# An expert stage written out over 16 pairs, with eight weight slots and gathers in the middle of the pairs

## The reference

```
def hier_moe(xn, w_rg, b_rg, w_re, b_re, w_gate, w_up, w_down):
    ...                       # top-1 of 4 groups, top-2 of 8 experts in it
    def expert_block(args):
        xb, e = args
        hdn = jax.nn.silu(xb @ w_gate[e]) * (xb @ w_up[e])
        return hdn @ w_down[e]
    ...
    y_sorted = y_pad[dest] * gate_flat[order][:, None].astype(y_pad.dtype)
    out = jax.ops.segment_sum(y_sorted, tok_sorted, num_segments=t)
```

## Time and profile before

| | us |
|---|---|
| median of three runs | 1980.41 |
| the profiled execution, its own time | 1979.28 |
| its span | 1977.5 |
| TensorE busy | 1767.3 (89%) |
| VectorE, ScalarE, GpSimd busy | 707.9, 669.3, 666.8 |
| DMA read | 524.25 MB, mean 266 GB/s over the span |

### The profile page before, as it was taken

How to read it: one execution, slowest core, us unless ns; L and a number is a source line. 1 busy time by engine, 2 the same in 40 slices (tenths; PEclk the granted TensorE clock), 3 DMA queues, 4 the chain that set the end, 5 groups by cost and what they waited for, 6 DMA issues and landing times.

```text
span 1977.5 us, 27621 instructions
## 1 busy us (share of the span) xinstructions
PE 1767.3 (89%) x8814; PEld 1074.9 (54%) x8814; DVE 707.9 (36%) x1299; ACT 669.3 (34%) x1300; POOL 666.8 (34%) x537
## 2 busy tenths in 40 slices
PE   6999999996988989889779999999969889898897
PEld 5789666785333333333267896667853333333432
DVE  5538667323112121121255385773241121211211
ACT  4565555653111111111145555566421011110200
POOL 6688565893000000000066885558920000000000
PEclk9999999997999999999989999999979999999999
DMA  7344221463799998989553541215538989989895
GB/s 282 128 171 171 86 69 60 154 272 143 310 427 382 429 430 363 428 373 430 252 214 134 193 172 58 86 43 205 222 128 359 427 366 430 429 374 428 358 429 243
DMA packets 38022, 526.77 MB, mean 266 GB/s; under 512 B 4232, under 2 KB 5016, under 8 KB 6160
## 3 DMA queue, kind: packets, MB, share of 16 engines
q1 hardware_dynamic: 37504, 523.74, 64.9%
q0 software_dynamic: 400, 1.59, 0.2%
HBM read 524.25 MB, written 1.06 MB: 266 GB/s over the span
## 4 chain that ended last, share of the span: by engine, by line
PE 37%; issue 35%; POOL 13%; DMA 8%; DVE 4%; ACT 1%; POOLq 0%; DVEq 0%; SPq 0%; ACTq 0%
POOL view L1738 12%; PE PS L968 9%; DMA view<-in_w_exp_up_dram 8%; PE PS L995 3%; PE PS L651 3%; PE PS L653 3%; PE PS L652 3%; PE PS L785 2%; PE PS L943 2%; PE PS L745 2%; PE PS L746 2%; PE PS L747 2%; DVE view L1430 2%; PE PS L820 1%; PE PS L794 1%
## 5 line engine op out<-in xcount | busy, mean ns | idle before, releaser
L1738 POOL TENSOR_TENSOR view<-view,view 128x512 fp32r<-128x512 f32 x448 | 578.1, 1311 | 667.3 <-ACT view L1028 662.3
L968 PE MATMUL PS<-view,view 128*64 128x512 f32 x2048 | 466.1, 612 | 62.7 <-DMA view<-in_w_exp_up_dram 41.5
L968 PEld LDWEIGHTS PS<-view,view 128*64 128x64 f32 x2048 | 151.5, 141 | 371.8 <-issue 371.8
L1028 ACT ACTIVATE view<-view 128x512 fp32r<-128x512 f32 x448 | 273.7, 628 | 206.4 <-PE PS L653 189.6
L651 PE MATMUL PS<-view,view 128*128 128x512 f32 x704 | 295.5, 420 | 8.9 <-POOL view L1738 8.6
L653 PE MATMUL PS<-view,view 128*128 128x512 f32 x704 | 275.4, 391 | 0.0
L652 PE MATMUL PS<-view,view 128*128 128x512 f32 x704 | 275.1, 391 | 0.0
L995 PE MATMUL PS<-view,view 128*64 128x512 f32 x1024 | 234.6, 612 | 6.3 <-ACT view L1257 6.3
L1670 DVE TENSOR_TENSOR view<-PS,view 128x512 f32<-128x512 f32 x32 | 22.1, 692 | 498.5 <-PE PS L968 498.5
L651 PEld LDWEIGHTS PS<-view,view 128*128 128x128 f32 x704 | 133.2, 189 | 46.9 <-POOL view L1738 13.2
L652 PEld LDWEIGHTS PS<-view,view 128*128 128x128 f32 x704 | 133.3, 189 | 32.8 <-issue 8.2
(11 more groups left out here) (242 smaller groups left out, 1988.1 us busy)
## 6 DMA issues: line engine op xcount, KB each, us to landing
view<-in_w_exp_gate_dram SPq DMA_DIRECT2D x64, 2048.0 KB, 16.6
view<-in_w_exp_up_dram SPq DMA_DIRECT2D x64, 2048.0 KB, 15.9
view<-in_w_exp_down_dram SPq DMA_DIRECT2D x64, 2048.0 KB, 14.8
view<-in_w_mix_dram SPq DMA_DIRECT2D x56, 2048.0 KB, 7.8
view<-bias_table POOLq DMA_DIRECT2D x1, 1536.0 KB, 15.1
view<-in_x_dram SPq DMA_DIRECT2D x1, 1024.0 KB, 4.9
out_dram<-view SPq DMA_DIRECT2D x1, 1024.0 KB, 4.7
dtw<-in_w_dt_dram SPq DMA_DIRECT2D x2, 256.0 KB, 5.1
```

The costliest lines, as they stand in the source:

```text
L968: ins = pe.matmul(bank(ph, name, j)[s * CAP:(s + 1) * CAP, :], xgT[:, k, (2 * j + s) * CAP:(2 * j + s + 1) * CAP], slot8[first + s][:, k, ...
L1028: nc.scalar.activation(highs(chunk), weights(slot8, chunk), ACT.Copy).then_inc(*high_ready.up(ph))
L1738: g_.tensor_tensor(weights(low8, chunk), weights(slot8, chunk), highs(chunk), ALU.subtract).then_inc(*low_ready.up(ph))
```

## The change

1. The expert part is no longer a loop over four units. Each engine has the 16 pairs of a layer written out, in the same layer program as the mixer (`first_pass` on TensorE); all their fills stand in `MIX_PLAN`. The units remain for the extra passes only, with semaphores of their own (`over_...`).
2. Eight weight slots that rotate: load n goes to slot `ORDER[n % 8]` and is issued once the product that used load n - 8 is complete. The two new slots lie in the memory of hT and the sigmoids (`r_h`, `r_g`) and in that of the bias table and M (`r_bt`, `r_m`). Hence the bias table is loaded anew in each layer, by the sync engine, within the mixer.
3. Gathers are for four experts (256 columns, `HALF`). Those of the next four stand in the middle of a pair, 16 matmuls in each of two pairs, between the first scatter and the transposes of hh. A fill holds two of the eight k blocks; the banks are 7 and 2, and ScalarE copies out the even fills and VectorE the odd ones. VectorE makes the selection ahead, at the start of each even pair.
4. `vectors` for the next layer moves behind load 16; the mixer's first blocks wait for the last g and u instead of u and y2.
5. In the branch not taken VectorE alone raises the semaphores, 27 of them.

```diff
+def gathered(j):
+    return (2 * (j % 2), 2 * (j % 2) + 1) if j // 2 + 1 < HALVES else ()
...
+ORDER = (4, 5, 1, 2, 0, 3, 6, 7)
...
+        slot_at = [region(SLOT) for _ in range(6)]
+        r_h, r_g, r_bt, r_m = region(2 * D), region(2 * D), region(HEADS * 384), region(1024)
+        slot_at += [r_h, r_bt]
...
                 for i, src in enumerate(blocks):
                     if i < RING:
-                        sp.wait_ge(*filled[1 if i < 2 else 4].at(ph, 0))
+                        sp.wait_ge(*filled[0 if i else 1].at(ph, 0))
...
+                    if i == RING + 1:
+                        sp.wait_ge(*filled[4].at(ph, 0))
+                        sp.wait_ge(s_skew, 16)
+                        sp.dma_start(BT, bass.AP(table_dram.tensor, 0, [[1, P], [WIN, HEADS], [1, 384]])
+                                     ).then_inc(*bt_in.up(ph))
...
+                sp.wait_ge(*full(ph, "lg"))
+                load(1, 0, 0)
+                load(1, 0, 1)
+                for n in range(SLOTS, 6 * ALL_PAIRS):
+                    sp.wait_ge(*used(n - SLOTS))
+                    load(n // 6, n % 6 // 2, n % 2)
+                    if n == 2 * SLOTS and not last:
+                        sp.wait_ge(*flag_ready.at(ph, 1))
+                        vectors(l + 1, Phase(l + 1))
...
-                for j in range(1, PAIRS):
-                    pair(first, j)
-                with sp.Fori(1, GROUPS) as g:
-                    unit(Phase(l, g, g))
...
+            def first_pass(ph):
+                def gather(h, i):
+                    key = ("xg", h, i)
+                    if i == 0:
+                        pe.wait_ge(*S_ready.at(ph, h + 1))
+                    pe.wait_ge(*free(ph, *key))
+                    for k in (2 * i, 2 * i + 1):
+                        for t in range(TT):
+                            for part in (XNh, XNl):
+                                ins = pe.matmul(bank(ph, *key)[:, (k % 2) * HALF:(k % 2 + 1) * HALF],
+                                                part[:, t, k * P:(k + 1) * P], S2[h % 2][:, t, :],
...
+                    ins.then_inc(*fill(ph, *key))
...
+                for j in range(ALL_PAIRS):
...
+                    if j:
+                        scatter(ph, j - 1, 0)
+                    for i in gathered(j):
+                        gather(h + 1, i)
+                    pe.wait_ge(*out_of(ph, "u", j))
+                    pe.wait_ge(*free(ph, "hh", j))
+                    for k in range(FF // P):
+                        ins = pe.transpose(PS[:, 2, k * P:(k + 1) * P], hh[:, k * P:(k + 1) * P], ident[:, :])
...
+                select(0)
+                for i in (1, 3):
+                    gathered_out(0, i)
+                for j in range(ALL_PAIRS):
+                    if j % 2 == 0 and j // 2 + 1 < HALVES:
+                        select(j // 2 + 1)
+                    gated(ph, j)
+                    for i in gathered(j):
+                        if i % 2:
+                            gathered_out(j // 2 + 1, i)
+                    if j:
+                        add(ph, j - 1)
+                    scaled_low(ph, j)
```

More of the change, by code:

```diff
@@ L307, in encoder @@
         S = view(r_q, TT, PER_GROUP * CAP, dt=F32R)
+        S2 = [view(r_q + i * 512, TT, HALF, dt=F32R) for i in range(2)]
+        Sg2 = [view(r_q + 1024 + i * 512, TT, HALF) for i in range(2)]
         XNl = view(r_xn, TT, D, dt=F32R)
@@ L318, in encoder @@
         xgT = view(r_x, KD, PER_GROUP * CAP)
-        BT = view(region(HEADS * 384), HEADS, 384)
+        xgT2 = [view(r_x + i * 2 * D, KD, HALF) for i in range(2)]
+        BT = view(r_bt, HEADS, 384)
         r_w = region(2 * D)
@@ L447, in encoder, with fills, drains @@
         POOL_CONSTS = 10
+        def fills(ph):
+            return filled if ph.unit is None else over_filled
+        def drains(ph):
+            return drained if ph.unit is None else over_drained
         def fill(ph, *key):
             bank, n = ph.plan(key)
-            sem_ = filled[bank].up(ph)
-            assert ph.made[filled[bank]] == n, key
+            sem_ = fills(ph)[bank].up(ph)
+            assert ph.made[fills(ph)[bank]] == n, key
             return sem_
@@ new lines, in layer, with scatter @@
+                    all_passed(pe, over_drained, Phase(l, UNITS - 1))
+            def scatter(ph, j, t):
+                for n in range(2):
+                    pe.wait_ge(*out_of(ph, "y2", j, n))
+                    pe.wait_ge(*out_of(ph, "G", j))
+                    pe.wait_ge(*free(ph, "s", j, t, n))
+                    o, pick_t = bank(ph, "s", j, t, n), Gm[:, t * P:(t + 1) * P]
+                    pe.matmul(o, pick_t, yeh[:, n, :], start=True, stop=False)
+                    pe.matmul(o, pick_t, yel[:, n, :], start=False, stop=True
+                              ).then_inc(*fill(ph, "s", j, t, n))
@@ new lines, in layer, with gated @@
+                    for s in range(6):
+                        dve.sem_inc(over_loaded[s].sem, UNITS * PAIRS * 16)
+                    for of in (over_S, over_Sg, over_yeh, over_step):
+                        dve.sem_inc(of.sem, UNITS * of.unit)
+                    dve.sem_inc(shifted.sem, PASSES - 1)
+            def gated(ph, j):
+                dve.wait_ge(*full(ph, "u", j))
+                dve.wait_ge(*out_of(ph, "g", j))
+                dve.wait_ge(*before(ph, "hh", j))
+                v.tensor_tensor(hh, PS[:, 1, :], silug, ALU.mult).then_inc(*drain(ph, "u", j))
@@ new lines, in add, with scaled_low @@
+            def add(ph, j):
+                for t in range(TT):
+                    for n in range(2):
+                        x_ = X[:, t, n * COLS:(n + 1) * COLS]
+                        dve.wait_ge(*full(ph, "s", j, t, n))
+                        v.tensor_tensor(x_, bank(ph, "s", j, t, n), x_, ALU.add
+                                        ).then_inc(*drain(ph, "s", j, t, n))
+            def scaled_low(ph, j):
+                yeh_done = yeh_ready if ph.unit is None else over_yeh
+                dve.wait_ge(*out_of(ph, "G", j))
+                for n in range(2):
+                    dve.wait_ge(*full(ph, "y2", j, n))
+                    dve.wait_ge(*yeh_done.at(ph, 2 * j + n + 1))
+                    v.scalar_tensor_tensor(out=yel[:, n, :], in0=PS[:, 3 + n, :], scalar=gcol[:, 0:1],
+                                           in1=yeh[:, n, :], op0=ALU.mult, op1=ALU.subtract
+                                           ).then_inc(*drain(ph, "y2", j, n))
```

352 lines of the change are left out of this document (220 added, 132 removed).

## The result

The changed kernel takes 1918.34 us (median; 1916.68 to 1922.67) against 1980.95 of the kernel before on the same chip: ratio 0.9688 [0.9668, 0.9709]. The forecast was 1907, its range 1898 to 1936. The time lies inside the range; the forecast is 11 us too fast. The profiled execution was the slowest of its four, 1922.67 us, so between profiles the gain is 56.6 us where 73.4 were forecast.

The account below looks back on a forecast made before the run. Weight transfers at 430 GB/s were taken to bound the expert stages. Gains of 32.7 + 37.2 + 1.3 + 2.2 = 73.4 us from the profiled 1979.3 give 1905.9, plus 1.1 for the median 1907.0; range 1898 to 1936.

Parts of the forecast that it names:

- What bounds the stage: Expert stages: weight transfers at 430 GB/s are the bound, 29.3 us per pair of experts against 24.7 us on TensorE.
- a cover of 12 us: First expert stage: TensorE's work takes 444 us from pair 0, the stream 456.5, leaving 12 us of cover.
- The sign that pairs would be 29.3 us apart: Sign of being right: in the expert stage pairs start 29.3 us apart, TensorE waiting for gate and up weights in most.
- A: Rival, expert stage: TensorE becomes the bound, new wait and clock losses making a pair 30.5 us; 1941 us, chance 0.15.
- B: Rival, expert stage: short waits hold TensorE's clock low, pair 32.2 us; 1987 us, deciding below clock 0.87; chance 0.06.
- C: Rival, expert stage: sync engine issues strictly in turn, queue empty 1 us per pair, 28 us lost; 1935 us, chance 0.07.
- Start of pair 0 in the first layer: First expert stage: smaller selection and gather let pair 0 start 5.0 us earlier, at 494.4.
- The stream in the first layer: First expert stage: 88 loads of 4.88 us take 429.4 us; stage ends at 950.9, a gain of 32.7 us.
- Between the layers: Boundary to the second layer: earlier mixer loads move casts away, 1.8 us, less 0.5 us for VectorE's branch; gain 1.3 us.
- I take 0.5 us more (nothing to 1.5): VectorE's branch between the layers, 6.13 us before: 27 counts replacing 8 waits and 13 counts add 0.5 us.
- The second stage: Second expert stage: pair 0 at 1477.4, end at 1932.2 against 1969.4, a gain of 37.2 us.
- The end: End of the kernel: VectorE's last adds themselves release the output instead of later counts, a gain of 2.2 us.

## Why the prediction was right, and where it was off

**What bounds the stage: right.** The DMA rate has no dips, TensorE alone needs 445.5 us in both layers (half weights) against 444 forecast, a pair 27.83 against 27.9, and doubling the gather turns the bound over, as a cover of 12 us said it would. The sign that pairs would be 29.3 us apart with a wait for weights in most of them does not hold: six of the sixteen pairs of the first layer have one, none before 728.85. I had forgotten that eight loads of head start are used up first.

**Rivals.** A is refuted by those runs, with 12.6 us of waits for weights in the first layer. B: the granted clock in the stages is 0.98 and 0.99. The bound of 0.87 given for B was a slip: 26.4 us of work and 1.5 of waits reach the stream's 29.3 already at a clock of 26.4 / 27.8 = 0.95, so the margin against B was smaller than stated, though the measured clock is above it too. C: no dip once a pair. One argument against A does not stand: that clock losses follow from waiting for weights. The runs with doubled gathers and with half weights never wait for weights and have such products all the same (7.88 to 8.68 us and 7.87 to 8.16 instead of 7.09).

**Where the 16.8 us went** that the profiled execution took beyond 1905.9, term by term:

- Start of pair 0 in the first layer, 3.6 us (497.95 against 494.4). Gather, copies and selection gave 4.4 of the 5.0 us: 3.5 between gather start and pair 0 (10.7 to 7.2), 0.6 for the selection, 0.3 for loop entry. The router at the lower clock took 2.65 us of that (4.39 to 7.04), the mixer ended 1.3 us later (transposes at 469.24 against 467.98), and the steps between router and selection were 0.9 us shorter. Why the mixer ended later isn't tested.
- The stream in the first layer, 3 us: from pair 0 it took 459.6 instead of 456.5. At the mean of 426.5 instead of 430 GB/s 88 loads need 433 us, not 429.4. Some 25 packets of instructions now pass from 505 to 940 us, and one slice fell to 395; what share each has isn't shown.
- Between the layers, 2.9 us. The casts gave 1.85 where 1.8 was forecast, but TensorE's gap grew by 3.4. The failed step is "I take 0.5 us more (nothing to 1.5)": the branch grew by 2.8, and without the arm and its counts it is 3.9 shorter. The steps from VectorE's copy to the transposes grew by the other 0.6 (990.50 to 997.34, now 967.18 to 974.62): up to the norm they grew by 1.6, beside GpSimd's split of the weights (the first two took 0.82 and 0.98 us, 0.25 and 0.16 in the kernel before), and from the norm on they shrank by 1.0. The forecast put the earlier loads down as gain alone.
- The second mixer, 3.6 us: it grew by 2.6, its router at 1432.60 again 7.04 us against 4.33, where the forecast took 0.95 off its end for selection and loop entry. The clock was watched in the stage and not ahead of it.
- The second stage, 2.5 us: stream 1.9 (456.7 against 454.8), gather and copies 0.6 (7.3 us from gather to pair 0 against 6.7).
- The end, 0.9 us: the output is issued 2.3 us sooner after the last add, where 2.2 was forecast, but takes 6.0 us from issue to the span's end, where it took 5.0.

The sum is 16.5 us. In medians the miss is smaller, 11 us, since the profiled execution lay 4.3 above its own and the forecast had added 1.1 for the median.

**Which part of the change earned it.** Two slots are 20 us in the stages and 5 between the layers, the latter with the mixer loads that go out later when there are six; in medians it is 28 to 29. Mid-pair placement is 0 (two pairs of runs). The other 33 to 34 us of the 62.6 stay with six slots and gathers at the start of a pair (1946.39 against 1980.31 on the same chip). What is left to explain them is four experts per gather instead of eight, the selection made ahead, no group boundary, and the other small moves of the change. Their split among these wasn't run, nor was the kernel before with eight slots alone.

## What to carry to other kernels

A consumer that is faster than its stream on average keeps the queue of weights full when its longest round, from one use of a slot to the next, takes about as long as the loads in flight or less. Six loads are 29.3 us: rounds of 36.1 us left dips of 5.5 to 7.6 us, rounds of about 29.7 left none, and where the stop stood within them did not matter. More slots beyond that are a head start, worth their own transfer time once per stage. Price first what stands between the stages: semaphore counts in the arm of a branch that runs, small VectorE operations beside a busy GpSimd, and the granted clock of short matmul groups after an idle stretch. Branch and clock each cost here about as much as the largest error inside the stage.

## What the hardware showed beside

- One core's DMA stream held 423 to 432 GB/s, but for one slice, over 400 us of straight code, with 41 instruction packets between 470 and 980 us. The Trainium skill, DMA: Bandwidth & Descriptors, section Where 436 GB/s comes from, puts the bound for reads from HBM at about 358 GB/s a core; this trace, of one core at work, stays above it throughout.
- An arm of a branch with 27 semaphore counts: 3.9 us on VectorE (8.94 to 5.02).
- VectorE operations on 128x2 elements took 1.18 and 1.19 us while GpSimd worked and 0.17 as soon as it was done.
- VectorE left a branch 6.9 us later when three loads of weights were issued 10.6 us later (copy at 974.12 against 967.18).
- The same 32 router matmuls took 3.76 us at a granted clock of 1.00 and 7.04 at 0.50, and from 3.97 to 7.04 in runs with the same router code.
